# Order of the query strips and of the older head's sums, and where the modulation rows are computed

## What is computed

```python
# second layer: 16 heads, two score maps of 64 dimensions each, values of 128
attn = p[:, :, 0] - lam * p[:, :, 1]
o = rms_norm(einsum(attn, v), subln_g) * (1.0 - lam_init)
y = (o * silu(g)) @ w_out

# last two layers: 8 query heads of 128 dimensions over 2 key/value heads
q = rope(rms_norm(q, q_norm)); s = q @ k.T * scale; o = softmax(s) @ v
y = concat([sgu * silu(za), merge_heads(o) * silu(zb)]) @ w_out
x = x + gate * y
```

## Time and profile before

| | |
|---|---|
| three executions | 2798.18, 2798.53, 2805.46 us |
| the profiled execution | 2805.79 us |
| its span | 2804.1 us |
| TensorE matmul busy | 2639.0 us, 94% |
| TensorE weight loads (beside the matmuls) | 2133.3 us, 76% |
| VectorE busy | 2045.8 us, 73% |
| ScalarE busy | 1224.6 us, 44% |
| POOL busy | 211.6 us, 8% |
| chain that ended last, by engine | PE 75%, DVE 12%, issue 5%, DMA 4%, ACT 3% |

### The profile page before, as it was taken

One profiled execution on the slowest core, in us unless ns is written; L12 is line 12 of the kernel. 1 busy time (PEld: TensorE's weight loads), 2 busy tenths in 40 slices (PEclk: granted clock), 3 DMA queues, 4 the chain that ended last, 5 costly groups with the idle time before them and its releaser, 6 DMA issues.

```text
span 2804.1 us, 39539 instructions
## 1 busy us (share of the span) xinstructions
PE 2639.0 (94%) x13490; PEld 2133.3 (76%) x13490; DVE 2045.8 (73%) x3196; ACT 1224.6 (44%) x1875; POOL 211.6 (8%) x402
## 2 busy tenths in 40 slices
PE   5799999999899999999989899999998997999989
PEld 1477777788677777777768788888886887998978
DVE  4399999999778788687877777764454666775655
ACT  3266556622443444444345433323444324544642
POOL 1110011011000000000000011100000100110000
PEclk8799999999999999999999899999999998999999
DMA  9765455476455565565655355532221643873325
GB/s 370 287 196 164 166 181 177 145 262 225 180 180 204 178 199 181 183 209 195 217 187 193 131 188 182 187 123 99 68 74 49 223 148 124 282 239 120 122 101 167
DMA packets 126557, 498.35 MB, mean 178 GB/s; under 512 B 14464, under 2 KB 16512, under 8 KB 116608
## 3 DMA queue, kind: packets, MB, share of 16 engines
q1 hardware_dynamic: 74176, 267.49, 27.7%
q0 software_dynamic: 52288, 229.66, 23.8%
HBM read 492.90 MB, written 4.19 MB: 177 GB/s over the span
## 4 chain that ended last, share of the span: by engine, by line
PE 75%; DVE 12%; issue 5%; DMA 4%; ACT 3%; DVEq 1%; POOL 0%; ACTq 0%; POOLq 0%; SPq 0%
PE psum L249 18%; PE psum L251 18%; PE psum L250 18%; PE psum L262 4%; DMA y<-in_mod_weights 2%; DVE w_lo L231 2%; PE psum L263 2%; DVE psum L409 2%; PE psum L299 2%; ACT w_hi L223 1%; PE psum L1631 1%; PE psum L1099 1%; PE psum L836 1%; DVE work L411 1%; PE psum L1645 1%
## 5 line engine op out<-in xcount | busy, mean ns | idle before, releaser
L249 PE MATMUL psum<-h_both,w_hi 128*128 128x512 f32 (+1 forms) x3264 | 1184.3, 363 | 5.6 <-DVE w_lo L231 5.6
L251 PE MATMUL psum<-h_both,w_lo 128*128 128x512 f32 (+1 forms) x3264 | 1156.1, 354 | 0.0
L250 PE MATMUL psum<-h_both,w_hi 128*128 128x512 f32 (+1 forms) x3264 | 1155.4, 354 | 0.0
L231 DVE TENSOR_TENSOR w_lo<-raw,w_hi 128x1024 fp32r<-128x1024 f32 x496 | 584.9, 1220 | 305.3 <-ACT w_hi L223 302.4
L249 PEld LDWEIGHTS psum<-h_both,w_hi 128*128 128x128 f32 x3264 | 619.6, 190 | 100.0 <-issue 13.2
L250 PEld LDWEIGHTS psum<-h_both,w_hi 128*128 128x128 f32 x3264 | 619.8, 190 | 92.4 <-issue 9.8
L251 PEld LDWEIGHTS psum<-h_both,w_lo 128*128 128x128 f32 x3264 | 619.1, 190 | 85.8
L223 ACT ACTIVATE w_hi<-raw 128x1024 fp32r<-128x1024 f32 x496 | 496.7, 1052 | 388.3 <-PE psum L251 301.4
L262 PE MATMUL psum<-h_both,w_hi 128*128 128x512 f32 x480 | 177.0, 409 | 10.0 <-DVE h_both L609 9.6
L263 PE MATMUL psum<-h_both,w_lo 128*128 128x256 f32 x480 | 137.0, 286 | 0.0
L409 DVE SCALAR_TENSOR_TENSOR psum<-y,modraw 128x1024 f32<-128x1024 f32 x98 | 120.3, 1228 | 21.1 <-DMA y<-in_mod_units 18.5
(11 more groups left out here) (289 smaller groups left out, 3127.3 us busy)
## 6 DMA issues: line engine op xcount, KB each, us to landing
raw<-in_weights SPq DMA_DIRECT2D x496, 512.0 KB, 4.4
y<-in_mod_units POOLq DMA_DIRECT2D x130, 512.0 KB, 4.2
modraw<-in_mod_weights POOLq DMA_DIRECT2D x48, 1024.0 KB, 5.5
work<-in_mod_units POOLq DMA_DIRECT2D x62, 512.0 KB, 4.6
y<-in_mod_weights POOLq DMA_DIRECT2D x16, 1024.0 KB, 9.1
xl<-in_mod_units POOLq DMA_DIRECT2D x32, 512.0 KB, 4.8
modraw<-in_mod_units POOLq DMA_DIRECT2D x32, 512.0 KB, 4.7
modraw<-in_cond_rows POOLq DMA_DIRECT2D x6, 1024.0 KB, 8.0
```

The lines of the kernel that those rows point to most:

```text
L231: dve.tensor_tensor(w_lo[:, par, half, :], raw[:, 2 * par + half, :], w_hi[:, par, half, :].bitcast(F32), ALU.subtract).then_inc(S["split_ ...
L249: pe.matmul(dst, hi, h_hi[:, k, 0:n], start=(k == 0), stop=False)
L250: pe.matmul(dst, hi, h_lo[:, k, 0:n], start=False, stop=False)
L251: mm = pe.matmul(dst, lo, h_hi[:, k, 0:n], start=False, stop=(k == KT - 1))
```

## The change

It has three parts.

1. In the first attention the sums of the older head stand between the two halves of the key strip (where a chunk may not stand), and no longer behind the scores. On ScalarE the root of these sums comes before the evacuation of the key strip, and an exponential of one element behind it (`warm`), so a head has four table loads and not two.
2. `PLAIN_HEADS = 4`: heads 0 to 3 have no chunks, no turns and no adds; heads 4 to 15 keep two chunks each, two groups fewer in all. Heads 1 to 8 have six half-units each instead of four, in places of 1, 2, 1 and 2. POOL's first chunk load is issued in its round of head 4.
3. In the grouped attention the query strip of head i+1 comes ahead of the gate strip of head i, in the program and in the weights' order. A head's steps are one round behind its query strip and not two.

Of the grouped attention's two bodies the diff shows what stands there now, and leaves out the statements that went; those are in the print above.

```diff
@@ -58,13 +58,14 @@
 MOD_FIRST = 8
 M_ATT = MOD_FIRST
-MOD_GROUPS = M_ATT + HEADS1 // 2
-AT_ATT = 28
+PLAIN_HEADS = 4
+MOD_GROUPS = M_ATT + (HEADS1 - PLAIN_HEADS) // 2
+AT_ATT = 30
 
 U_OUT0 = 2 * BLOCKS
 U_ATT = U_OUT0 + KT
-U_GATE1 = U_ATT + KT
+U_GATE1 = U_ATT + KT + KT // 2
...
-        ATT_UNITS = [0] + [4] * 8 + [0] + [6, 6, 6, 6, 4, 4]
+        ATT_UNITS = [0] + [6] * 8 + [0] + [6, 6, 6, 6, 4, 4]
...
-            at = ATT_AT[ATT_UNITS[i]]
+            at = [1, 2, 1, 2] if i < 9 and ATT_UNITS[i] else ATT_AT[ATT_UNITS[i]]
...
             def chunk_in(n):
-                if n < 2 * HEADS1:
+                n -= 2 * PLAIN_HEADS
+                if 0 <= n < 2 * (HEADS1 - PLAIN_HEADS):
                     mod_load(pool, M_ATT + n // 4, n % 4)
...
-            chunk_in(0)
...
+                if i == PLAIN_HEADS:
+                    chunk_in(2 * i)
                 chunk_in(2 * i + 1)
                 after(i, 0)
-                chunk_in(2 * i + 2)
+                if i >= PLAIN_HEADS:
+                    chunk_in(2 * i + 2)
                 for place in range(1, 4):
                     after(i, place)
...
+                mods = not isinstance(i, int) or PLAIN_HEADS <= i < HEADS1
+                m = M_ATT + j - PLAIN_HEADS // 2
                 def chunk(n):
-                    return lambda half: mod_chunk(pe, M_ATT + j, 2 * par + n) if half else None
+                    return lambda half: mod_chunk(pe, m, 2 * par + n) if half and mods else None
+                def sums():
+                    pe.wait_ge(A["o_evac"], i - 1)
+                    pe.wait_ge(A["sdq"], min(i, HEADS1) if isinstance(i, int) else i)
+                    pe.matmul(psum[:, M_BANK, 0:T], ones, osq, start=True, stop=True).then_inc(A["sso"], 1)
+                def key_strip(half):
+                    if half and mods:
+                        mod_chunk(pe, m, 2 * par)
+                    elif not half and older:
+                        sums()
                 first = isinstance(i, int) and i == 0
                 last, end = (isinstance(i, int) and i == HEADS1 + n for n in range(2))
...
-                    strip(pe, att_strip(j, par, 0), psum[:, K_BANK, :], NT, chunk(0))
+                    strip(pe, att_strip(j, par, 0), psum[:, K_BANK, :], NT, key_strip)
...
-                if older:
-                    pe.wait_ge(A["o_evac"], i - 1)
-                    pe.matmul(psum[:, M_BANK, 0:T], ones, osq, start=True, stop=True).then_inc(A["sso"], 1)
+                if older and not here:
+                    sums()
...
-                    if par:
-                        mod_turn(pe, M_ATT + j, 1)
+                    if par and mods:
+                        mod_turn(pe, m, 1)
...
+                def root():
+                    act.wait_ge(A["sso"], i - 1)
+                    act.activation(osq, psum[:, M_BANK, 0:T], ACT.Sqrt, scale=1.0 / P, bias=eps_col).then_inc(A["sdo"], 1)
+                if older and here:
+                    root()
+                    act.activation(warm, eps_col, ACT.Exp)
                 if here:
...
-                if older:
-                    act.wait_ge(A["sso"], i - 1)
-                    act.activation(osq, psum[:, M_BANK, 0:T], ACT.Sqrt, scale=1.0 / P, bias=eps_col).then_inc(A["sdo"], 1)
+                if older and not here:
+                    root()
...
-                        mod_add(dve, M_ATT + j, at=AT_ATT + j)
+                    if par and i >= PLAIN_HEADS:
+                        mod_add(dve, M_ATT + j - PLAIN_HEADS // 2, at=AT_ATT + j - PLAIN_HEADS // 2)
...
-        def gqa_strip(lay, j, par, c):
-            return Strip(S_NET2 + lay * L2_STRIPS + L2_ATT, 2 * par + c, j, 4)
+        def q_strip(lay, j, par):
+            first = isinstance(j, int) and 2 * j + par == 0
+            return Strip(S_NET2 + lay * L2_STRIPS + L2_ATT, 0 if first else 2 * par - 1, j, 4)
+        def z_strip(lay, j, par):
+            last = isinstance(j, int) and 2 * j + par == HEADS2
+            return Strip(S_NET2 + lay * L2_STRIPS + L2_ATT, 2 * par - 1 if last else 2 * par, j, 4)
...
             def body(j, par):
                 i = 2 * j + par
+                here, before = live(i, HEADS2), live(i - 1, HEADS2)
+                first, second, end = (isinstance(i, int) and i == m for m in (0, 1, HEADS2))
+                if here:
+                    ge(pe, B["q_evac"], base + i)
+                    strip(pe, q_strip(lay, j, par), psum[:, 0, 0:n], n, (lambda half: None if half else turned(0)) if second else None)
+                if second:
+                    scores(0, 0)
+                if before and not second and not end:
+                    turned_weights(i - 1)
+                if here:
+                    sums(i)
+                if before:
+                    ge(pe, B["sz"], base + i - 1)
+                    strip(pe, z_strip(lay, j, par), psum[:, 1, 0:n], n)
+                if second or end:
+                    turned_weights(i - 1)
+                if end:
                     pe.wait_ge(B["q_evac"], base + HEADS2)
                     pe.wait_ge(B["sz"], base + HEADS2)
                     out_first(pe, 2 + lay, 0, 4)
+                if here and not first:
+                    turned(i)
+                if before:
+                    weighted(i - 1, 1 - par)
+                if here and not first:
+                    scores(i, par)
                 if end:
+                    out_first(pe, 2 + lay, 4, OUT_REST)
+            rounds(pe, body, HEADS2, 1, 4)
...
             def body(j, par):
                 i = 2 * j + par
+                here, before = live(i, HEADS2), live(i - 1, HEADS2)
+                first, second, end = (isinstance(i, int) and i == m for m in (0, 1, HEADS2))
+                if before and not second:
+                    exps(i - 1)
                 if here:
+                    st = q_strip(lay, j, par)
                     act.wait_ge(S["strip_done"], st.s + 1)
                     next_strip(split_hi, act, st)
                     ge(act, B["qr"], base + i)
+                    if first:
                         act.wait_ge(B["v_t"], 2 * (lay + 1))
                     act.activation(q2[:, 0:n], psum[:, 0, 0:n], ACT.Copy)
                     act.activation(q2s[:, 0:n], psum[:, 0, 0:n], ACT.Square).then_inc(B["q_evac"], 1)
+                if second:
+                    exps(0)
+                if before and not second and not end:
+                    weights(i - 1)
                 if here:
+                    act.wait_ge(B["ssq"], base + i + 1)
+                    act.activation(q2s[:, 0:n], psum[:, 6, 0:n], ACT.Sqrt, scale=1.0 / P, bias=eps_col).then_inc(B["sdq"], 1)
+                if before:
+                    st = z_strip(lay, j, par)
                     act.wait_ge(S["strip_done"], st.s + 1)
+                    if end:
+                        split_hi(act, st.pair + 1, st.par, halves=(0,))
+                        to_high(act, 2 + lay, 0, 1)
+                        split_hi(act, st.pair + 1, st.par, halves=(1,))
+                        to_high(act, 2 + lay, 1, 3)
+                        weights(i - 1)
+                        to_high(act, 2 + lay, 3, 4)
+                        gate(i - 1, 1 - par)
+                        to_high(act, 2 + lay, 4, OUT_REST)
+                    else:
+                        next_strip(split_hi, act, st)
+                        gate(i - 1, 1 - par)
+                if second:
+                    weights(0)
+            rounds(act, body, HEADS2, 1, 4)
...
-             + [c for h in heads for c in (q + h, zb + h)])
+             + [q + heads[0]] + [c for n in range(1, HEADS2) for c in (q + heads[n], zb + heads[n - 1])] + [zb + heads[-1]])
```

More of the change, by code:

```diff
@@ L1587, in body @@
             def body(j, par):
                 i = 2 * j + par
-                here, before, older = live(i, HEADS2), live(i - 1, HEADS2), live(i - 2, HEADS2)
-                last, end = (isinstance(i, int) and i == HEADS2 + n for n in range(2))
-                if last:
+                here, before = live(i, HEADS2), live(i - 1, HEADS2)
[3 more added lines that the diff above has]
+                    strip(pe, q_strip(lay, j, par), psum[:, 0, 0:n], n, (lambda half: None if half else turned(0)) if second else None)
@@ L1617, in body @@
-                if here:
-                    ge(pe, B["sz"], base + i)
-                    strip(pe, gqa_strip(lay, j, par, 1), psum[:, 1, 0:n], n)
-                    pe.wait_ge(B["q_evac"], base + i + 1)
-                    ge(pe, B["sdq"], base + i)
-                    pe.matmul(psum[:, 6, 0:n], ones, q2s[:, 0:n], start=True, stop=True).then_inc(B["ssq"], 1)
-                if last:
-                    out_first(pe, 2 + lay, 8, 10)
-                if end:
-                    out_first(pe, 2 + lay, 14, OUT_REST)
@@ L1657, in body, with gate @@
+            def gate(h, par):
+                ge(act, B["y2"], base + h - 1)
```

(51 more changed lines are left out.)

252 lines of the change are left out of this document (117 added, 135 removed).

## The result

| | before | changed |
|---|---|---|
| median, executions beside each other | 2803.4 us (2798.2 to 2807.2, 6 runs) | 2819.1 us (2816.6 to 2824.4, 6 runs) |
| span of the profiled execution | 2804.1 us | 2822.7 us |

The ratio is 1.0057 with a 95% interval of 1.0044 to 1.0069: the change makes the kernel 16 us slower. By the traces, whose spans are 18.6 us apart, it gains 16 us in the first attention and loses 34 in the two grouped attentions. The table takes stages from these two traces, in us; its marks are the square of head 0's and of head 4's keys, the first product of the reciprocal roots in the next layer's normalization, and the copy of the second values ahead of a grouped attention. "Low" is the time with a granted clock of 0.50, which is 1.2 GHz.

What follows compares the result with a forecast made beforehand. The prediction took TensorE to set the time everywhere. First attention -10 and grouped attention +28 (48.3 + 17 - 37.3) gave +18 us: 2816 against the median 2798.5; the 8-in-10 range was 2797 to 2835.

Steps and rivals of the forecast that it cites:

- 2802: Rival for the grouped attention: the clock holds through the twelve 2.2 us waits, only the longest pay; 2802 us, chance 0.17.
- 2777: Rival for the grouped attention: the sums don't wait for the squares, twelve waits and their clock drops go; 2777 us, chance 0.07.
- 2835: Rival: all 17 grouped-attention waits bring the low clock (+11), VectorE's waits stay in heads 1 to 3 (+8); chance 0.15.
- 2832: Rival in the first attention: the root stays late and the key sums wait as before; +16, 2832 us, chance 0.07.
- Key sums: First attention: TensorE's wait before the key sums goes, 18.6 us in 14 heads, 1.33 each.
- the cut strip's cost: First attention: cutting the key strip in two costs between 0 and 0.3 us a head, 2 us in all.
- Heads 0 to 3: First attention: without chunks TensorE alone gains 13.3 us, but head 4's late chunk leaves these heads 2 us slower.
- The queue behind the eighteenth half-unit: POOL issues head 4's chunk after head 3's last half-unit load: VectorE through at 909.3, chunk at 915, TensorE stands some 13 us.
- The step that VectorE keeps up: Heads 5 to 8 of the first attention: VectorE needs about 42 us a head, TensorE 44.5 less 1.3.
- Waits of the grouped attention: New TensorE waits of 48.3 us: 37.2 in the heads, including twelve of 2.2, and 11.1 at the ends.
- Clock: Grouped attention: five in eight of 17 waits bring the low clock at 1.65 us each; 17 us new, 8.3 old.
- Table loads: First attention: ScalarE's two more table loads a head, 1.28 us each, cost nothing; no added drain of about 1.38 us.

Runs made afterwards that it cites:

- e3: The changed kernel with POOL's load of head 4's first chunk issued before the unit loads of heads 1 to 3: 2805.6 us, ratio 1.0004.
- e6: The kernel before with the second part alone (no chunks in heads 0 to 3, six half-units in heads 1 to 8): 2825.1 us, ratio 1.0072.
- e9: The kernel before with the second part alone, and head 4's first chunk loaded early: 2816.7 us, ratio 1.0053.
- e2: The changed kernel with ScalarE's copy and square of a query strip ahead of the split: 2791.4 us, ratio 0.9963 to the kernel before.
- e7: The changed kernel with three products of 256 columns ahead of each grouped-attention head's wait for the square: 2812.2 us, ratio 1.0028 to the kernel before.
- e8: The kernel before with the first part alone (older head's sums in the key strip), first chunk's load where it was before: 2786.6 us, ratio 0.9936.

## Why the prediction was right, and where it was off

The forecast was +18 us, 2816: -10 in the first attention and +28, mostly new waits, in the grouped attentions. Measured were +16, 2819; the kernel before took 2803.4 us in six executions, where the forecast started from 2798.5. In the stages it is -15.8 and +34.4. The mechanisms came as forecast, and the rivals' times (2802, 2777, 2835, 2832) were not met. But both halves were about 6 us larger than priced, in opposite directions, and that the total still came within 3 us is luck.

*Key sums.* Right: no wait is left in 14 heads. **Off: the cut strip's cost.** I took 2 us in all. From head 5's to head 15's keys (starts of L1165 and now L1189) the ten periods fell from 448.9 to 433.6 us, 1.53 each against 1.28 to 1.36 of wait: the cut costs nothing, and 0.2 a head is gained beside the wait, for which no cause is shown.

*Heads 0 to 3.* The queue behind the eighteenth half-unit came as described: VectorE through at 907.6 (forecast 909.3), load issued at 908.2, chunk at 914.2 (forecast 915), TensorE standing 13.6 us (forecast 13). TensorE's gain up to there was 12.6 (forecast 13.3). e3 shows that the stand is this load alone. The early units cost next to nothing only because the root had moved (e6, e9). The step that VectorE keeps up held for the changed kernel, but the prediction priced the two parts singly and did not see that the second needs the first.

*First attention in all.* Forecast -10, measured -15.8: heads 0 to 4 are 1.6 longer, against a forecast of 2 and 2 more for the clock; the others are 17.4 shorter, against a forecast of 16 less 2.

*Waits of the grouped attention.* Forecast 48.3 us, in the trace 46.7, partly by luck: six of 1.8 to 1.9 in each layer (forecast 2.2), 3.1 and 2.7 for head 0's sums (forecast 3.4 and 3.0), 0.6 and 1.0 for head 1's (1.1 and 1.7), 5.8 and 4.5 at the ends (forecast 6.3 and 4.8). All these are shorter than forecast, and 3.8 and 2.8 before head 0's weighted values, which I had not seen, make up for it. The twelve are shorter, in layer 0, because the turned weights cover 1.5 us (2012.90 to 2014.37 above), where I took 1.2. e2 shows the split as their cause.

*Clock.* **Off: its size.** The forecast had 17 us for new stretches less 8.3 for old ones, 8.7 net; the measured growth of TensorE's busy time is 13.0. The changed kernel's two stages have 48 us at 1.2 GHz, before it was 17. Of the twelve waits of 1.84 to 1.92 us seven brought the low clock (two of six in layer 0, five of six in layer 1), near the five in eight that I took. Of the six waits of 2.7 to 5.8 us five brought it, and two of these stretches lasted 6.8 us and not 3.4. The rest of the 34.4 us is idle time: forecast 48.3 less 29, 19.3 net, measured 21.5. The earlier trace rows had pointed the right way against the rule of the Trainium skill (TensorE: Matmul & The Clock Gate, Why this matters for your kernels) that a short pause leaves the clock up, and e7 shows it by filling the pauses. Why five of the twelve nearly equal waits left it up stays open.

*Table loads.* The row was right: 1.28 us, and the next activation 0.02 us behind (and 1084.92 above), without the drain that the Trainium skill adds (ScalarE: Activation LUTs, What ACT_TABLE_LOAD costs). That two more loads a head cost nothing was right too (e8).

## What to carry to other kernels

When a step is moved nearer to its producer, look at what stands ahead of the evacuation on the engine between: a split that prepares a later strip was free behind a whole strip, and behind a short cover nearly all of its 2.0 us turned into idle time of TensorE (1.84 to 1.92 us a head). Putting the evacuation first took 28 us back. A load that stands in one queue behind loads gated by another engine's progress comes as late as that engine; issuing it ahead of them took 13.5 us back. Two parts of a change can need each other: cost them together, with the chain that one lengthens and the other takes off the path.

## What the runs showed of the hardware

Idle stretches of TensorE as short as 1.84 us were followed by 1.2 GHz in seven cases of twelve. Three small products in each of the twelve left 0.5 to 0.6 us idle and kept the clock at 2.4 GHz behind them (e7; granted 0.99 over the windows instead of 0.97 and 0.93). The fourteen waits of 1.28 to 1.36 us before the key sums in the kernel before were never followed by it. A low stretch of 3.4 us lost 1.6: in layer 0 a head takes 31.7 us from sums to sums without one and 33.3 with one. So such a wait costs not 1.9 but some 2.8 us on the average, an estimate from 1.9 and seven twelfths of 1.6.
